# An attention seam rearranged: SP issues the small transfers, v is transposed before the old y, and takes come before the weighted sum

## What is computed

```python
q, k, v = split(u @ w_in, 3)                  # per head: q, k 2 x 64 wide, v 128 wide
q, k = apply_rope(q), apply_rope(k)
p = softmax(causal(q @ k.T / 8))              # for both halves c = 0, 1
a = p[:, :, 0] - lam_val * p[:, :, 1]
o = rmsnorm(a @ v, norm_g) * (1 - lam_init)   # over the 128 columns of the head
return o @ w_out
```

## Time and profile before

| | before |
|---|---|
| median of 3 runs | 2455.27 us |
| profiled execution, first to last instruction | 2453.2 us |
| PE busy | 2309.0 us, 94% |
| DVE, ACT, POOL busy | 1657.0, 888.9, 921.8 us |
| mean granted TensorE clock | 0.97 |
| attention of layer 1, first scores to the last old y | 1210 to 1716 us |

### The profile page before, as it was taken

The page is one execution under the profiler, slowest core; times in us unless marked ns, Lnnn a source line. Parts: engine busy times, 40 slices in busy tenths (PEclk is TensorE's granted clock), DMA queues, the critical chain, the costliest instruction groups (busy, mean ns, idle before and its releaser), DMA issues.

```text
span 2453.2 us, 28316 instructions
## 1 busy us (share of the span) xinstructions
PE 2309.0 (94%) x10601; PEld 1898.4 (77%) x10601; DVE 1657.0 (68%) x1956; ACT 888.9 (36%) x1471; POOL 921.8 (38%) x356
## 2 busy tenths in 40 slices
PE   7999997999999999998998999987999999999998
PEld 5788885777788888887777777765777788888887
DVE  7544436579939669398466666676579839669396
ACT  4131122235334243344144444444135334243345
POOL 5424336443323233231644444446442323233230
PEclk9999998999999999999999999998999999999999
DMA  6111111345271542700522222212345171442701
GB/s 175 43 35 34 43 34 52 120 154 206 69 268 58 189 172 69 269 23 34 147 58 55 52 59 60 59 36 68 112 154 206 69 274 54 187 172 69 274 1 69
DMA packets 128832, 262.61 MB, mean 107 GB/s; under 512 B 7217, under 2 KB 81122, under 8 KB 121314
## 3 DMA queue, kind: packets, MB, share of 16 engines
q1 hardware_dynamic: 122658, 243.34, 28.5%
q10 hardware_dynamic: 6080, 17.96, 3.0%
HBM read 202.56 MB, written 41.94 MB: 100 GB/s over the span
## 4 chain that ended last, share of the span: by engine, by line
PE 77%; DVE 12%; issue 3%; ACT 3%; DMA 2%; ACTq 1%; POOL 1%; DVEq 0%; SPq 0%; POOLq 0%
PE aps L865 9%; PE aps L869 9%; PE aps L867 9%; PE dps L765 5%; PE dps L767 5%; PE dps L766 5%; PE dps L869 3%; PE mps L869 3%; PE mps L865 3%; PE dps L865 3%; PE dps L867 3%; PE mps L867 3%; PE dps L747 2%; PE dps L749 2%; PE dps L748 2%
## 5 line engine op out<-in xcount | busy, mean ns | idle before, releaser
L618 POOL TENSOR_TENSOR w_hi<-w_raw,ones 128x1024 fp32r<-128x1024 f32 x64 | 164.9, 2577 | 520.2 <-PE dps L767 290.2
L765 PE MATMUL dps<-one_hi,w_hi 128*128 128x512 f32 x608 | 260.6, 429 | 12.1 <-DVE a_next L1583 12.1
L865 PE MATMUL aps<-b_ring,w_hi 128*128 128x512 f32 x640 | 252.6, 395 | 13.8 <-issue 13.8
L867 PE MATMUL aps<-b_ring,w_lo 128*128 128x512 f32 x640 | 251.7, 393 | 0.0
L869 PE MATMUL aps<-b_ring,w_hi 128*128 128x512 f32 x640 | 251.7, 393 | 0.0
L703 POOL TENSOR_TENSOR s_blk<-s_blk,a 128x1024 f32<-128x1024 f32 x32 | 93.6, 2926 | 409.0 <-DVE w_lo L1627 283.1
L767 PE MATMUL dps<-one_lo,w_hi 128*128 128x512 f32 x608 | 242.4, 399 | 0.0
L766 PE MATMUL dps<-one_hi,w_lo 128*128 128x512 f32 x608 | 241.6, 397 | 0.0
L1645 DVE TENSOR_TENSOR b_ring<-h,b_ring 128x1024 fp32r<-128x1024 f32 x120 | 222.3, 1861 | 7.5 <-ACT b_ring L1248 7.5
L622 POOL TENSOR_TENSOR w_lo<-w_raw,w_hi 128x1024 fp32r<-128x1024 f32 x64 | 160.1, 2501 | 5.0
L747 PE MATMUL dps<-one_hi,w_hi 128*128 128x512 f32 x384 | 153.4, 399 | 6.9 <-DVE m_next L1583 3.6
(11 more groups left out here) (292 smaller groups left out, 5619.1 us busy)
## 6 DMA issues: line engine op xcount, KB each, us to landing
b_ring<-xs SPq DMA_DIRECT2D x42, 2048.0 KB, 7.9
xs<-b_ring SPq DMA_DIRECT2D x14, 2048.0 KB, 7.4
a<-in_w_up SPq DMA_DIRECT2D x16, 1024.0 KB, 5.3
a<-in_w_down SPq DMA_DIRECT2D x16, 1024.0 KB, 7.5
w_raw<-in_mlstm_w_in SPq DMA_DIRECT2D x24, 512.0 KB, 4.0
w_raw<-in_diff_w_in SPq DMA_DIRECT2D x24, 512.0 KB, 3.8
hspill<-h SPq DMA_DIRECT2D x2, 4096.0 KB, 13.3
h<-hspill SPq DMA_DIRECT2D x16, 512.0 KB, 3.6
```

The costliest lines, as they stand in the source:

```text
L618: nc.gpsimd.tensor_tensor(w_hi[:, slot], w_raw[:, slot], ones[:, :].unsqueeze(1).broadcast_to([P, NT, P]), ALU.mult).then_inc(pool_chain, 1)
L765: nc.tensor.matmul(dps[:, half], w_hi[:, slot, k], rh, start=(k == 0), stop=False)
L865: nc.tensor.matmul(to[:, n], wh, ring[:, 0, k], start=new and k == 0, stop=False, skip_group_check=not new)
L867: nc.tensor.matmul(to[:, n], wl, ring[:, 0, k], start=False, stop=False, skip_group_check=not new)
```

## The change

DMAs. `swap_halves` and `repeat_q` move from ACT's program to SP's, word for word. They stand among the weight loads, in fixed places (`staged`): the load of panel 3hd+7 comes behind the copies of q of head hd and the swap of q of head hd+1, the load of panel 3hd+8 behind the swap of k of head hd+1.

Order at a seam. PE does the scores of block 0, v (which now waits for the last weighted sum's eviction, `o_out`), the last triples, two new triples, the scores of block 1, two triples, and only then the old y, which goes to the second halves of the score banks, `aps[:, 1]` and `aps[:, 3]`. These are first needed by the scores of block 4, which wait for them. ACT splits q a step earlier, in two pieces. DVE's order is in the rows below: its takes come ahead, `head_norm` after the new head's first mask and maximum, and `head_out` after the combination of block 1.

```diff
@@ SP
+            def staged(i, p):
+                if p % 3 == 1:
+                    if p == 1:
+                        repeat_q(2 * i - 2)
+                    else:
+                        repeat_q(2 * i - 1)
+                    swap_halves(2 * i - 1 + p // 3, 0)
+                elif p % 3 == 2:
+                    swap_halves(2 * i - 1 + p // 3, 1)
...
+                            if not first:
+                                staged(i, p)
+                            elif p >= 4:
+                                swap_halves(0, p - 4)
...
+                    if layer == 1 and p == 1:
+                        repeat_q(AH - 2)
+                        swap_halves(AH - 1, 0)
                     load_panel(g, g % 2, tiles(w, p * P))
+                if layer == 1:
+                    swap_halves(AH - 1, 1)
+                    repeat_q(AH - 1)
@@ PE
+                if m == 4 and not first:
+                    pe.wait_ge(oy_out, 2 * hd)
...
                 scores(hd, 0, first)
                 feed(FEED)
+                pe.wait_ge(evac, 2 * (G_MIX[1] + 3 * hd + 3))
                 if not first:
-                    attention_end(hd - 1)
-                    pe.wait_ge(oy_out, 2 * hd)
-                pe.wait_ge(evac, 2 * (G_MIX[1] + 3 * hd + 3))
+                    pe.wait_ge(o_out, 8 * hd)
...
-                    last = nc.tensor.transpose(mps[:, n // 4, (n % 4) * P:(n % 4 + 1) * P],
+                    last = nc.tensor.transpose(aps[:, 1 + 2 * (n // 4), (n % 4) * P:(n % 4 + 1) * P],
                                                o8[:, n], ident[:, :])
...
+            def attention_first(hd, feed, first=False):
+                feed(FEED_AT[0][0])
+                scores(hd, 1, first)
+                feed(FEED_AT[1][0])
+                if not first:
+                    attention_end(hd - 1)
+                values(hd, 0, feed, FEED_AT[1][1])
+                feed(FEED_AT[1][2])
...
+                attention_rest(hd, feed, lambda s, half: None, plan)
+                if last:
+                    attention_start(hd + 1, feed)
+                else:
+                    attention_start(hd + 1)
+                    feed(FEED)
+                attention_first(hd + 1, (lambda n: None) if last else head_feed(i, a + 1))
@@ ACT
+                if s == NB - 1 and more:
+                    split_q(hd + 1, 0)
+                act.wait_ge(pv_done, n + 1)
+                if m == 0 and follows:
+                    act.wait_ge(oy_done, hd)
...
+                if s == NB - 1 and more:
+                    split_q(hd + 1, 1)
@@ DVE
+                attention_rest(hd, feed, plan)
+                split_q(hd + 1)
+                feed(sum(plan[NB]))
+                split_k(hd + 1)
+                mask_and_max(hd + 1, 0)
+                if last:
+                    feed(FEED)
+                head_norm(hd)
+                combine(hd + 1, 0)
+                feed(FEED)
+                attention_first(hd + 1, (lambda n: None) if last else head_feed(hd + 1))
+                head_out(hd)
```

More of the change, by code:

```diff
@@ L1069, in attention_core, with attention_rest @@
+            def attention_first(hd, feed, first=False):
[6 more added lines that the diff above has]
+                feed(FEED_AT[1][2])
+            def attention_rest(hd, feed, early, plan=FEED_AT, first=False):
+                for s in range(2, NB + 1):
                     if s < NB:
-                        scores(hd, s)
+                        scores(hd, s, first)
@@ L1071, in attention_core @@
                     feed(plan[s][0])
                     early(s, 0)
[L1073 to L1092, removed]
+                    values(hd, s - 1, feed, plan[s][1])
                     feed(plan[s][2])
@@ L1438, in _, with split_q @@
             act.dma_start(sinb[:, :], sin_t).then_inc(cs_ld, 16)
[L1440 to L1450, removed]
+            def split_q(hd, c):
+                if c == 0:
+                    act.wait_ge(rot_ready, 2 * hd + 1)
+                nc.scalar.activation(q_hi[MAP[c], c], a_next[MAP[c], 0], ACT.Copy).then_inc(qk_hi, 1)
             def split_k(hd):
@@ L1483, in attention_start @@
                 last.then_inc(vt_ready, 1)
-            def attention_core(hd, more):
[L1486 to L1512, removed]
@@ new lines, in step @@
+            def step(hd, s, more=False, follows=True):
+                m, n = s - 1, 8 * hd + s - 1
+                for t in range(BATCHES[m]):
+                    u = BEFORE[m] + t
+                    k = min(3, m + 1 - 3 * t)
+                    act.wait_ge(t_done, BATCH * hd + u + 1)
+                    if m >= 1 and t == 0:
+                        act.wait_ge(pv_done, n)
+                    nc.scalar.activation(at[:, 3 * t:3 * t + k],
+                                         mps[:, u % 2, 0:k * P].rearrange("p (n d) -> p n d", d=P),
+                                         ACT.Copy).then_inc(t_out, 1)
+                if s < NB:
+                    exponentials(hd, s)
+                elif more:
+                    split_k(hd + 1)
[4 more added lines that the diff above has]
+                    act.wait_ge(oy_done, hd)
+                nc.scalar.activation(o8[:, m], mps[:, 0, 3 * P:4 * P], ACT.Copy,
+                                     scale=small[:, 11, m:m + 1])
+                nc.scalar.activation(acc[:, m % 2, 0:P], mps[:, 0, 3 * P:4 * P], ACT.Square,
+                                     scale=small[:, 11, m:m + 1],
+                                     accum_out=small[:, 3, m:m + 1]).then_inc(o_out, 1)
+                if s == NB - 1 and more:
+                    split_q(hd + 1, 1)
@@ L1513, in attention_core @@
+            def attention_core(hd, more):
+                for s in range(2, NB + 1):
+                    step(hd, s, more)
                 if more:
                     attention_start(hd + 1)
-            swap_halves(0, 0)
-            swap_halves(0, 1)
-            split_q(0)
+                    step(hd + 1, 1)
+            for c in range(2):
+                split_q(0, c)
             split_k(0)
-            repeat_q(0)
             attention_start(0)
+            step(0, 1, follows=False)
@@ L2092, in combine, with head_norm @@
                                                ee[:, 0, 0:w], ALU.mult, ALU.add).then_inc(comb_ready, 1)
[L2094 to L2102, removed]
+            def head_norm(hd):
                 dve.wait_ge(o_out, 8 * hd + 8)
@@ L2114, in attention_core, with attention_first, attention_rest, head_feed @@
                     nc.vector.tensor_scalar(flat(h[:, ds(hd, 1), half * HALF:(half + 1) * HALF]),
[L2115 to L2118, removed]
+                                            aps[:, 1 + 2 * half], again[:, 0:1], None, ALU.mult).then_inc(oy_out, 1)
+            def attention_first(hd, feed):
+                feed(FEED_AT[0][0])
+                mask_and_max(hd, 1)
+                combine(hd, 1)
+                feed(sum(FEED_AT[1]))
+            def attention_rest(hd, feed, plan=FEED_AT):
+                for s in range(2, NB):
+                    mask_and_max(hd, s)
+                    combine(hd, s)
+                    feed(sum(plan[s]))
+            def head_feed(hd, total=FEED):
+                return Feed(lambda u, v: attention_takes(3 * hd + 4, 1, u, v), total)
             attention_takes(0, 0, 0, 3 * 16)
-            split_qk(0)
+            split_q(0)
+            split_k(0)
             attention_takes(0, 0, 3 * 16, 4 * 16)
```

90 lines of the change are left out of this document (60 added, 30 removed).

## The result

The changed kernel takes 2426.1 us (median of four runs, 2425.8 to 2429.8) against 2456.0 (four runs) beside it: a ratio of 0.9883, with the interval 0.9871 to 0.9895. The forecast was 2431.6 in a range of 2414 to 2450. The profiled span is 2424.5 us against 2453.2, so 28.7 us went where 23.7 were forecast.

The account below looks back on a forecast made before the run. PE, busy 94% of the span, bounds the kernel by its work, idle time and low clock. 25.5 + 11.9 + 4.3 - 6 - 12 = 23.7 us less gives a span of 2429.5, runs 2.1 above: 2431.6 us, range 2414 to 2450.

Parts of the forecast that it names:

- 25.5 + 11.9 + 4.3 = 41.7 us: Gains: PE's waits at loop seams 25.5, full clock there 11.9, head 6's wait and slow stretch 4.3 us.
- a wait stays: Rival: at every seam a cover fails or copies land late; PE idles 1 to 2 us; 2450 us, chance 0.20.
- slower by the lock at each seam: Rival: DVE's norm falls under POOL's split in each loop seam, 33 us lost; 2465 us, chance 0.07.
- give some back: Loop heads: twelve DMA issues fewer per head on ACT offset some of block 2's delay; both put at nothing.
- the forecast of the clock: Full clock at loop seams, 11.9 us, and behind head 6's wait, 1.7 us.
- The forecast heads: Sign of being right: loop heads 59 to 60 us apart in place of 65.7.
- The term of 11.9 us: Loop seams: without PE idle time the clock stays up; five drops return 1.7 us each, one 3.4.
- Forecast +6: Start of head 0: copies of q stand behind a load waiting for POOL's split; PE starts 6 us later.
- the landing and the issues: Head 0: load's issue 0.5 us, four DMA issues 2.4, and 4.3 to land.
- 19 us of norm, PE idle some 17 us, net +12: Last seam: POOL's passes hold the norm's 12 instructions, 19 us in place of 3.4; 12 us lost.
- block 2 and on would meet POOL less: Last seam: block 0's map comes 13 us later, later blocks meet POOL less, so 12 us was taken.
- the rival of 2415.6: Last seam not held: DVE's small instructions slip through POOL's gaps; gain 39.7 us, chance 0.20.

Follow-up runs that it names:

- e5: Kernel before, with swaps and copies of q issued by SP; DVE's, ACT's and PE's order as before: 2450.6 us, 0.9988.
- e6: Changed kernel, with swaps and copies of q issued by ACT again, as before: 2437.8 us, 0.9935 to the kernel before.
- e8: Changed kernel, with ACT's split of q in one piece again, as before: 2430.2 us, 0.9901 to the kernel before.
- e7: Changed kernel, with DVE's take of the new panel's first half behind norm and combination in the loop: 2433.8 us, 0.9911 to the kernel before.
- e9: Changed kernel, with PE transposing the old y ahead of v and DVE's norm ahead of the mask: 2423.1 us, 0.9873 to the kernel before.
- e3: Changed kernel, with SP's copies of q ahead of the load that waits for POOL's split: 2421.8 us, 0.9865 to the kernel before.
- e1: Changed kernel, with POOL's 12 last-seam passes waiting until head 6's norm is done: 2411.4 us, 0.9825 to the kernel before.
- e2: Changed kernel, with head 6's norm on DVE ahead of the mask and the take of v: 2409.8 us, 0.9819 to the kernel before.

## Why the prediction was right, and where not

**Loop seams and clock.** Forecast: 25.5 + 11.9 + 4.3 = 41.7 us. Measured by the ledger: 6.4 + 37.4, and 11.8 less the 4.7 by which v's wait at the last seam fell (5.46 to 0.79), together 50.9, or 50 without the shift of y. All three mechanisms are in the trace: no wait for `h` or for the take, full clock at each seam, no 2.54 us in head 6. The rivals "a wait stays" and "slower by the lock at each seam" are out: DVE was through with the norm's small instructions at S+3.7, ahead of POOL's pass, and at all six seams with 0.5 to 0.7 us to spare.

**The step that was mis-sized here** is ACT's edits, which I put at nothing ("give some back"). I read three of PE's waits as those that matter, and passed over two that are larger than the 4.0 us for q_lo. The kernel before, whole span:

```profile
PE mps L1090 <- ACT at L1496: 9.1, 15, 2.5
PE mps L1084 <- ACT at L1496: 8.0, 16, 0.9
```

After, they are 4.2 and 4.4: 8.5 us less, of which the forecast had 2.5, in head 6. The DMA issues taken off ACT brought down the first (e5, e6), the split of q in two pieces the second (e8). From head 0's scores to v of head 7, before and after, columns as in the earlier trace rows:

```profile
1210.01:1667.41 457.40, 408.13 (x2168) 338.04 (x2169) 308.72 (x624) 200.92 (x543) 214.08 (x85) 0.96 0.22 55
1217.08:1618.85 401.77, 389.48 (x2161) 328.70 (x2161) 300.73 (x605) 201.42 (x543) 204.63 (x81) 0.99 0.24 61
```

PE's idle time fell from 49.3 to 12.3 us, by 37.0. Without the 4.7 us of v's wait, that is 32.3 against 28.0 forecast. The 4.3 us more are 6.0 for ACT's copies and 0.9 for q_lo at the last seam, less 2.7 of new waits for combinations. PE's busy time fell by 18.6 us, of which 1.0 is y's shift and 13.6 the forecast of the clock. The other 4.0 fit the tails of the waits: a matmul of 0.39 us starts 0.23 us behind the one before it, so each wait adds 0.16 us of busy time to its idle time, and 29 waits went. That is an estimate of mine, 4.6 us.

The Trainium skill's "DMA: Bandwidth & Descriptors", section "Issuing engines are not separate DMA queues", says that starting DMAs on several engines saves issue time only. The runs agree in kind; I took "only" for nothing, and four issues of 0.6 us each, twice a head, were something. The forecast heads were 59 to 60 us; they are 57.2 to 58.8. The longer ones, heads 3 and 4, hold a new wait: in head 3, DVE and POOL show

```profile
1424.91 3.25 DVE L2145 SCALAR_TENSOR_TENSOR ee<-ee,small 128x768 f32<-128x768 f32 x1
1428.08 0.29 DVE L2133 TENSOR_TENSOR aps<-aps,mask_qk 128x128 f32<-128x128 f32 x1
...
1424.96 2.38 POOL L703 TENSOR_TENSOR a_next<-a_next,swap 128x1024 f32<-128x1024 f32 x1
```

where the same combination takes 1.02 us in head 2, and PE waits 1.28 us. I had not looked for it.

**The clock.** The term of 11.9 us rests on idle time as the cause of the drops. The runs agree and sharpen it: with 1.34 us idle at the seam (e7) or 1.71 (e9) the clock stays at 1.00; with both, as before and in e5, it falls to half. So either of the two moves gives the clock back, beside the rest of the change.

**Head 0.** Forecast +6, measured +8.5 (e3: 8.2). The mis-sized terms are the landing and the issues. From the load's issue to the end of the last copy's it took 3.6 us (1207.84 to 1211.44), where I had 2.9. The copy came 5.6 us behind that end, where I put 4.3; counted as in the earlier trace rows, from the start of its issue, it is 6.6 us. The DMA engines were busy at 0.82 in that stretch, with the next weights and the swaps in flight; no run separates these.

**The last seam.** Forecast: 19 us of norm, PE idle some 17 us, net +12. Measured: 19.5 us, 17.84, and 21.2 - 4.7 = 16.5 net, 15.5 without the shift of y. The mechanism and the passes per instruction were right, and so was the map: from v to the map's transpose it took 3.2 us before and 21.8 after; with the 4.7 us of v's wait taken off, that is 13.9 us later, against 13 forecast. What I mis-sized is behind the map, where I took 1 us back since block 2 and on would meet POOL less. From there to the last old y, before and after:

```profile
1670.62:1714.72 44.10, 36.37 (x190) 28.67 (x190) 29.76 (x66) 22.18 (x67) 30.75 (x13) 0.89 0.25 72
1640.61:1687.40 46.79, 36.68 (x190) 28.78 (x191) 30.41 (x70) 21.99 (x67) 16.91 (x7) 0.86 0.12 35
```

It takes 2.7 us more, and the clock is not the reason, though the half clock lasts 27.3 us at this seam against 13.7 before: PE is busy only 0.3 us more. It is idle 2.4 us more, in waits for combinations (2.5 us against 0.2). The longest, DVE's row and PE's:

```profile
1643.09 2.34 DVE L2145 SCALAR_TENSOR_TENSOR ee<-ee,small 128x256 f32<-128x256 f32 x1
1645.49 0.69 PE L1115 MATMUL mps<-ident,ee 128*128 128x128 f32 x2 [1.93 <-DVE ee L2145]
```

The same instruction took 0.48 us in head 4, with POOL idle; here it stands beside a pass (1642.80 to 1645.15). Had I taken POOL's lock as absent, the rival of 2415.6 would have been the forecast: e1 and e2, where nothing is held, gave 2411.4 and 2409.8.

So 23.7 became 28.7 by errors that partly cancel, and by luck to that extent: some 8 us more in the loop, 6 lost beyond the forecast at the two ends, and 2.9 us gained ahead of attention and behind it.

## What to carry to other kernels

Work that is moved for a loop is also moved at the loop's ends: price the first and the last pass apart, since here these two gave back 24 of the 50 us that the loop won. Ahead of a burst of GpSimd passes, put DVE's small SBUF instructions first, or make the burst wait for them; their number counts, not their size (an instruction of 8 columns cost a whole pass of 2.4 us). And measure the edits of a bundle each against both ends: what was worth 3 us alone was worth 7 (by the traces) to 13 (by the medians) in company of the others.

## What the runs showed of the hardware

- Single-source and two-source DVE instructions of 128x8 in SBUF took 1.83 to 2.26 us beside POOL's passes and 0.17 us without. In 19.5 us of back-to-back passes 8 of 12 were held. A take from PSUM beside the first of these passes kept its 0.69 us.
- A single idle time of PE of 1.3 to 1.7 us per head didn't bring the lower clock; 1.71 and 1.99 us some 3 us apart did, for 3.4 to 6.8 us.
- Four DMA issues of 32 partitions hold ACT for 2.44 us and SP for 2.45, or 2.96 right behind the copies of q at head 0.
